# Two query tiles computed with the keys, the values a third tile later, and the conv taps' diagonals written early

## The chip, the cores and the metric

The kernel runs on one core of a Trainium2 chip. The metric is the device time in microseconds of one execution; lower is better. Every matrix product is done in fp32r with operands split in a high and a low part: three matmuls (high by high, high by low, low by high) for each product.

## The reference, cut to what matters

The program is two transformer blocks one after the other, on 256 tokens of width 1024 (the first block also carries 256 context tokens). The first block has two layers: a convolution layer and an attention layer. What the change touches is the attention layer's input side and the convolution's taps:

```
hx = rmsnorm(x, norm_g[i, 0]) * (1.0 + sc_x) + sh_x
hc = rmsnorm(ctx, norm_g[i, 0]) * (1.0 + sc_c) + sh_c
qx = apply_rope(rmsnorm((hx @ wq).reshape(B, S, N_HEADS, HEAD_DIM), q_g), cos, sin)
kx = apply_rope(rmsnorm((hx @ wk).reshape(B, S, N_KV_HEADS, HEAD_DIM), k_g), cos, sin)
kc = rmsnorm((hc @ wk).reshape(B, L, N_KV_HEADS, HEAD_DIM), k_g)
vx, vc = hx @ wv, hc @ wv
...
u = lax.conv_general_dilated(u, w_dw[:, None, :], ..., feature_group_count=u.shape[-1]) + b_dw
```

There are 16 query heads (1024 columns, eight tiles of 128) and 4 key and value heads (256 columns each). Keys and values are made from all 512 tokens, queries from the 256 of x alone.

## The kernel before, in words

**Weights.** All weights come as one stream of pieces of 128 by 1024 fp32 (512 KB), in an order written out in `stream_blocks`. SyncE loads them into seven buffers (`raw`). Pieces of ordinary weights are split: ScalarE copies a piece to fp32r (`whi`, `hi_to`, L1240), then VectorE (`lo_to`, L1908) or GpSimd (L2876, in four operations of 256 columns) writes the rest (`wlo`). `on_pool` decides which of the two, by the piece's turn and by the tile it belongs to. There are five buffers of each part, so a piece can be converted only when the piece five turns earlier has been used up by TensorE (`wdone`). A `raw` buffer is free once the low part is written. Pieces of `w_mod` (the modulation, names such as A, T0, T1) are not split; TensorE reads them from `raw` (L591), and a piece gives its buffer back then. `mod("A")` in the stream is 12 such pieces.

**The attention layer's input.** VectorE and ScalarE make the modulated normalised input k by k, for eight slices of the width: VectorE L2084 (scale), ScalarE L1314 (high part `Hh`), VectorE L2094 (low part `Hl`); VectorE also writes the last additions of the residual there (L2072), and GpSimd adds them to X (L2907). TensorE's `lin_first` (L513, L514: the two products with the high part; L519: the product with the low part) takes each k as soon as it is there, for several output tiles at once. In the kernel before it does so for the two key tiles, `("k", 0)` and `("k", 1)`, 512 tokens wide. Then `lin_tok` (L566 to L568) computes the values for four tiles of tokens. Then the keys' mean squares (`head_sums`, L623), then the eight query tiles, 256 tokens wide, one after the other (`q_lin`, L540 to L542), with the keys' reciprocal roots spread over 128 rows (`head_spread`, L858) behind the first of them, and small matmuls for the queries' mean squares (`q_sums`, L877) between the others.

**Leaving PSUM.** ScalarE's `head` copies a tile to SBUF (L1491 for a key, L1493 for a query) and squares it (L1495). VectorE scales the keys (`scaled`, L2319), turns keys and queries (`rope1`: L2324, L2325, L2327, L2329), and writes the low parts (L2359 for K1l, `q_lo` L2341); ScalarE writes the high parts (L1518 for K1h, `q_hi` L1500). GpSimd copies K1h and K1l to the other half of the partitions (L2922), after its last `wlo` of the queries. The softmax's row maxima on VectorE (L2399) stand in its queue behind the low part of query 7. Matrix products use five PSUM banks in turn.

**The convolution.** TensorE applies 30 taps of four of the eight channel tiles by diagonal 32 by 32 matrices (L767). GpSimd writes these (L2900) in four chunks of up to eight taps; there are three buffers, and the fourth chunk waits until TensorE has used the first.

Of the kernel before, what the change touches and what calls it, by code (L numbers as in the profile page):

```python
# [49 lines left out]
def stream_blocks():  # L50
# [201 lines left out]
def build(nc, wstream, vecs_d, const_d, xin, out):  # L252
# [13 lines left out]
    with ctx:  # L266
# [60 lines left out]
        slots.place(-1, "conv", "bank", range(4, 8), [b[:, :] for b in banks[4:8]])  # L327
        slots.place(0, "dg", "dg", range(3), [DG[:, i, :, :, :] for i in range(3)])
        slots.place(0, "rt", "rt", range(2), [rtb[:, i, :] for i in range(2)])
# [97 lines left out]
        def on_pool(s):  # L427
            tag = turn_tag.get(s, "")
            if s in [tile_turn[key] + 5 for key in (("wo2", 0, 7), ("wo2", 1, 7), ("down2", 0, 1, 7))]:
                return True  # L430
            if tag == "wo" and s <= tile_turn["q", 7] + 5:
                return False
            if tag in ("wo", "wo2", "down2"):
                return True
            if tag == "q":
                return s % 3 != 2
            if tag in ("z", "ya", "gate", "mz", "mb"):
                return s % 3 == 0
            if tag == "up2":
                return s % 3 == 2  # L440
            return False
# [30 lines left out]
        def tensor(e):  # L472
# [22 lines left out]

            def lin_first(keys, kt, src, n, high, low, until=None, between=lambda k: None, idle=0):
                got = [bank("pm", ("lin",) + key, *(until(key) if until else [("ev",) + key])) for key in keys]
                warm(got[0], idle)
                for k in range(kt):
                    xh, xl = src(k)  # L500
                    held = []
                    for ti, key in enumerate(keys):
                        p, o, last = block("w")
                        hi, lo = (x[:, turn_of[p] % NPIECE, o:o + 128] for x in (whi, wlo))
                        turn_tag.setdefault(turn_of[p], key[0])
                        for key_ in keys:
                            tile_turn[key_] = turn_of[p]
                        held.append((p, last, hi))
                        dst = got[ti][:, 0:n]
                        w.wait_ge(*on("lo", p))  # L510
                        for point in high(k):
                            w.wait_ge(*on(*point))
                        e.matmul(dst, hi, xh, start=k == 0, stop=False)  # L513
                        e.matmul(dst, lo, xh, start=False, stop=False)  # L514
                    for point in low(k):
                        w.wait_ge(*on(*point))
                    for ti, key in enumerate(keys):
                        p, last, hi = held[ti]
                        i = e.matmul(got[ti][:, 0:n], hi, xl, start=False, stop=k == kt - 1)  # L519
# [32 lines left out]

            def lin_tok(key, kind, n, tiles, src, xon, until):
                got = [bank("pm", ("lin", key, s), *until(s)) for s in range(tiles)]
                for k in range(8):
# [8 lines left out]
                    for s in range(tiles):  # L564
                        xa, xb = xh[:, s * 128:(s + 1) * 128], xl[:, s * 128:(s + 1) * 128]
                        e.matmul(got[s][:, 0:n], xa, hi, start=k == 0, stop=False)  # L566
                        e.matmul(got[s][:, 0:n], xb, hi, start=False, stop=False)
                        i = e.matmul(got[s][:, 0:n], xa, lo, start=False, stop=k == 7)  # L568
                        points = ([("wdone", p)] if last and s == tiles - 1 else []) + ([("lin", key, s)] if k == 7 else [])
                        if points:  # L570
                            i.then_inc(sig("pe_lin", *points), 1)


# [184 lines left out]
            for i_ in range(CONV_PE):  # L758
                c, q = i_ // CHUNK, i_ % CHUNK
                w.wait_ge(*on("dg", c))  # L760
                dg = DG[:, c % 3, :, :, :]
                for ct in range(4):
                    if i_ == 0:
                        w.wait_ge(*on("u", 4 + ct))
                    for r in range(4):
                        rows = slice(32 * r, 32 * r + 32)
                        i = e.matmul(two(got[r][32 * ct:32 * ct + 32, :]), dg[rows, ct, q, :], U[rows, 4 + ct, :, i_:i_ + T],  # L767
                                     start=i_ == 0, stop=False)
# [78 lines left out]

            def head_sums(key, n):
                b = bank("pst", ("stat", key), ("root", key))
                w.wait_ge(*on("sq", key))  # L850
# [14 lines left out]
            q_done = {}  # L865

# [362 lines left out]
        def scalar(e):  # L1229
# [252 lines left out]
            for k in range(8):  # L1482
                modulated("n2", 1, 0, 2, k)


# [15 lines left out]

            hi_to(("k", 0))
            for m in range(2):
                head(("k", m), 512)
            hi_to(("v",), 3)
            for m in range(2):
                root(("k", m), 8, ("wide", ("k", m)))
            for s in range(4):
# [3 lines left out]
            for j in range(8):  # L1512
                hi_to(("q", j))
                head(("q", j), T)
                if j == 2:
                    for m in range(2):
                        w.wait_ge(*on("roped", ("k", m)))
                        e.activation(K1h[:, 2 * m, :], slots.at(("hr", ("k", m))), ACT.Copy).then_inc(sig("act_q", ("k1h", m)), 1)  # L1518
                if j >= 2:
                    q_hi(j - 2)  # L1520
            w.wait_ge(*on("sums", "q"))
# [374 lines left out]
        def vector(e):  # L1896
# [446 lines left out]

            lo_to(("k", 0))
            lo_to(("v",), 3)
            for m in range(2):
                widen(("k", m), 512)
            for j in range(8):
                lo_to(("q", j))
                if j == 0:  # L2350
                    for m in range(2):
                        scaled(("k", m), 512, "attn_k_g")
                elif j == 1:
                    for m in range(2):
                        rope1(("k", m))
                elif j == 2:
                    for m in range(2):
                        w.wait_ge(*on("k1h", m))
                        e.tensor_tensor(K1l[:, 2 * m, :], slots.at(("hr", ("k", m))), f32(K1h[:, 2 * m, :]), ALU.subtract).then_inc(  # L2359
                            sig("dve_q", ("k1l", m)), 1)  # L2360
                if j >= 2:
                    rope1(("q", j - 2))
                if j >= 2:
                    q_lo(j - 2)
            rope1(("q", 6))
            q_lo(6)
# [496 lines left out]
        def gpsimd(e):  # L2863
# [30 lines left out]
            for c, (i0, n) in enumerate(CHUNKS):  # L2894
                for u in slots.take(0, "dg", ("dg", c), ("dgused", c)):
                    w.wait_ge(*u)
                dg = DG[:, c % 3, :, :, :]
                taps = vec("conv_w_dw", i0 * 8, n * 8).rearrange("p (q k) -> p q k", k=8)
# [224 lines left out]
```

## Time and profile before

| | |
|---|---|
| median of 3 runs | 1968.23 us (1968.08 to 1978.76) |
| profiled execution | 1963.36 us |
| its span, first to last instruction | 1961.1 us |
| TensorE busy | 1884.1 us, 96% of the span |
| VectorE, ScalarE, GpSimd busy | 1204.8, 956.5 and 525.0 us |
| mean granted TensorE clock | 0.992 of full speed |
| stage from the first key matmul to the first softmax maximum | 623.13 to 692.03 us |

The span is what the rows of the trace are counted in, from the first instruction; the profiled execution's time is 2.3 us longer than its span. TensorE is the engine of which the others are the servants here: what matters is when it stands, and who was late.

### The profile page before, as it was taken

How to read it: one execution, taken by the hardware profiler on the slowest of the kernel's cores; microseconds unless marked ns; L12 is line 12 of the kernel's file. 1: busy time of each engine (PE TensorE's matmuls, PEld its weight loads, DVE VectorE, ACT ScalarE, POOL GpSimd, SP SyncE). 2: the span in 40 equal slices, each digit the busy share in tenths (PEclk: the TensorE clock that was granted, in tenths of full speed). 3: DMA queues.
4: the chain of work that ended last, by engine and by line, in shares of the span. 5: the costliest groups of instructions: out<-in, count | busy, mean ns of one | idle time of the engine just before them, and what ended most of it. 6: DMA issues, size and time to landing. Idle time of an engine off the chain costs nothing.

```text
span 1961.1 us, 36041 instructions
## 1 busy us (share of the span) xinstructions
PE 1884.1 (96%) x14682; PEld 1666.9 (85%) x14682; DVE 1204.8 (61%) x2444; ACT 956.5 (49%) x1713; POOL 525.0 (27%) x668
## 2 busy tenths in 40 slices
PE   6999999999998989999998999999999899999998
PEld 3866778888885847899987989999999899999997
DVE  4998753233338575655578675685748876567474
ACT  4314532232233476544446564565655556456464
POOL 1110100000001443000011322647373322374736
PEclk9999999999999999999999999999999999999999
DMA  9345442222224255555544344555554544545551
GB/s 351 127 151 182 143 161 97 97 97 97 97 97 161 87 206 196 200 184 183 183 161 173 130 138 160 173 165 177 190 175 151 173 150 130 171 151 178 185 178 63
DMA packets 84547, 307.24 MB, mean 157 GB/s; under 512 B 9376, under 2 KB 10656, under 8 KB 84128
## 3 DMA queue, kind: packets, MB, share of 16 engines
q1 hardware_dynamic: 84384, 304.94, 45.9%
q8 instruction: 117, 1.92, 0.4%
q14 instruction: 46, 0.38, 0.1%
HBM read 303.86 MB, written 1.05 MB: 155 GB/s over the span
## 4 chain that ended last, share of the span: by engine, by line
PE 82%; DVE 9%; ACT 4%; issue 2%; DMA 1%; POOL 1%; SPq 0%; ACTq 0%; DVEq 0%; POOLq 0%
PE pb L540 18%; PE pb L542 17%; PE pb L541 17%; PE pb L513 6%; PE pb L514 6%; PE pb L519 6%; DVE wlo L1908 2%; PE pb L767 2%; DMA raw<-wstream 1%; ACT whi L1240 1%; PE pb L591 1%; POOL wlo L2876 1%; PE pb L927 1%; PE pb L1111 1%; PE pb L1124 1%
## 5 line engine op out<-in xcount | busy, mean ns | idle before, releaser
L540 PE MATMUL pb<-Hh,whi 128*128 128x256 f32 (+1 forms) x2304 | 699.6, 304 | 1.8 <-DVE SM L2501 1.6
L542 PE MATMUL pb<-Hh,wlo 128*128 128x256 f32 (+1 forms) x2304 | 692.5, 301 | 0.0
L541 PE MATMUL pb<-Hl,whi 128*128 128x256 f32 (+1 forms) x2304 | 692.5, 301 | 0.0
L1240 ACT ACTIVATE whi<-raw 128x1024 fp32r<-128x1024 f32 x468 | 489.7, 1054 | 319.4 <-PE pb L542 177.2
L1908 DVE TENSOR_TENSOR wlo<-raw,whi 128x1024 fp32r<-128x1024 f32 x328 | 424.5, 1298 | 346.4 <-ACT whi L1240 345.9
L2876 POOL TENSOR_TENSOR wlo<-raw,whi 128x256 fp32r<-128x256 f32 x560 | 418.1, 780 | 706.2 <-ACT whi L1240 705.3
L540 PEld LDWEIGHTS pb<-Hh,whi 128*128 128x128 f32 x2304 | 440.0, 191 | 23.0 <-DVE SM L2501 2.5
L541 PEld LDWEIGHTS pb<-Hl,whi 128*128 128x128 f32 x2304 | 440.2, 191 | 15.0
L542 PEld LDWEIGHTS pb<-Hh,wlo 128*128 128x128 f32 x2304 | 440.1, 191 | 15.0
L513 PE MATMUL pb<-Hh,whi 128*128 128x256 f32 (+1 forms) x528 | 162.6, 328 | 3.8 <-ACT Hh L1314 3.4
L514 PE MATMUL pb<-Hh,wlo 128*128 128x256 f32 (+1 forms) x528 | 160.0, 323 | 0.0
L2907 POOL TENSOR_TENSOR X<-X,tmpb 128x512 f32<-128x512 f32 x14 | 18.0, 1290 | 473.5 <-DVE tmpb L2072 473.5
L513 PEld LDWEIGHTS pb<-Hh,whi 128*128 128x128 f32 x528 | 103.2, 196 | 18.9 <-issue 8.9
L519 PE MATMUL pb<-Hl,whi 128*128 128x256 f32 (+1 forms) x528 | 106.7, 324 | 4.0 <-DVE Hl L2094 4.0
L514 PEld LDWEIGHTS pb<-Hh,wlo 128*128 128x128 f32 x528 | 103.2, 195 | 6.8
L519 PEld LDWEIGHTS pb<-Hl,whi 128*128 128x128 f32 x528 | 82.3, 194 | 14.1 <-DVE Hl L2094 6.9
L1875 ACT ACTIVATE tmpb<-pb,VEC 128x256 f32<-128x256 f32 x88 | 48.4, 564 | 79.1 <-PE pb L542 73.3
L2153 DVE SCALAR_TENSOR_TENSOR Y<-U,VEC,Y 128x512 f32<-128x512 f32 x120 | 81.8, 758 | 1.8 <-ACT Y L1355 1.8
L2835 DVE SCALAR_TENSOR_TENSOR tmpb<-pb,VEC,tmpb 128x255 f32<-128x255 f32 x88 | 42.3, 481 | 56.6 <-ACT tmpb L1875 55.6
L1450 ACT ACTIVATE tmpb<-pb 128x512 f32<-128x512 f32 (+1 forms) x44 | 21.1, 491 | 110.6 <-PE pb L542 97.3
L591 PE MATMUL pb<-raw,csz 128*32 128x512 f32 x384 | 52.9, 633 | 20.2 <-DMA raw<-wstream 19.6
L2270 DVE TENSOR_TENSOR tmpb<-pb,tmpb 128x512 f32<-128x512 f32 (+1 forms) x44 | 24.1, 557 | 59.8 <-PE pb L542 49.6
(335 smaller groups left out, 2956.5 us busy)
## 6 DMA issues: line engine op xcount, KB each, us to landing
raw<-wstream SPq DMA_DIRECT2D x572, 512.0 KB, 3.6
X<-xin SPq DMA_DIRECT2D x2, 1024.0 KB, 8.3
out<-X SPq DMA_DIRECT2D x8, 128.0 KB, 1.8
CON<-consts SPq DMA_DIRECT2D x1, 926.0 KB, 8.4
VEC<-vecs SPq DMA_DIRECT2D x1, 662.0 KB, 8.8
CON<-consts SPq DMA_DIRECT2D x1, 147.0 KB, 3.9
VEC<-vecs SPq DMA_DIRECT2D x1, 88.0 KB, 2.0
```

The costliest lines, as they stand in the source:

```text
L513: e.matmul(dst, hi, xh, start=k == 0, stop=False)
L514: e.matmul(dst, lo, xh, start=False, stop=False)
L519: i = e.matmul(got[ti][:, 0:n], hi, xl, start=False, stop=k == kt - 1)
L540: e.matmul(dst, hi, xh, start=k == 0, stop=False)
L541: e.matmul(dst, hi, xl, start=False, stop=False)
L542: i = e.matmul(dst, lo, xh, start=False, stop=k == kt - 1)
L591: i = e.matmul(dst[32 * c:32 * c + 32, :], csz[:, 4 * half + c, o:o + 32], raw[:, p % NRAW, (c % 2) * 512:(c % 2 + 1) * 512], start=m == h ...
L1240: e.activation(whi[:, s % NPIECE, :], raw[:, p % NRAW, :], ACT.Copy).then_inc(sig("act_hi", ("hi", p)), 1)
L1875: e.activation(t[:, s * T:(s + 1) * T], slots.at(("lin",) + key)[:, 0:T], ACT.Identity, scale=vec("ffn_conv_w_2", l * 132 + 88 + c), bias= ...
L1908: e.tensor_tensor(wlo[:, i, :], raw[:, p % NRAW, :], f32(whi[:, i, :]), ALU.subtract).then_inc(sig("dve_lo", ("lo", p)), 1)
L2153: e.scalar_tensor_tensor(out=y, in0=u, scalar=wt, in1=y, op0=ALU.mult, op1=ALU.add).then_inc(sig("dve_conv", *points), 1)
L2876: last = e.tensor_tensor(wlo[:, i, c:c + 256], raw[:, p % NRAW, c:c + 256], f32(whi[:, i, c:c + 256]), ALU.subtract)
```

## The change

Three things change.

1. The two first query tiles are computed in `lin_first` together with the keys, k by k; they take part with the first 256 of the 512 columns (`short`). Query tile 2 follows, then the mean squares of the keys, then the values, then query tiles 3 to 7. The keys' roots are spread inside the values' matmuls, behind their second k, instead of behind query 0. The stream's order is changed to match: keys and queries 0 and 1 in four pieces, then the 12 pieces of A, then query 2, the values (two pieces), queries 3 to 7. The queues of ScalarE and VectorE follow: ScalarE converts the pieces of query 2, the values and query 3 between the eight high parts of the input.
2. A third buffer for squares (`hq`), and the piece of query 2 is never GpSimd's.
3. The diagonals have a buffer for all four chunks, so GpSimd writes the fourth behind the third without a wait.

```
-    run([("attn_wk", (0,), m * 128) for m in range(2)], 2)
+    wq = [("attn_wq", (0,), m * 128) for m in range(8)]
+    group([("attn_wk", (0,), m * 128) for m in range(2)] + wq[:2])
+    mod("A")
+    group(wq[2:3])
     cols("attn_wv", (0,), 0, 256, 256)
-    mod("A")
-    run([("attn_wq", (0,), m * 128) for m in range(8)], 1)
+    for t in wq[3:]:
+        group([t])
...
-        U, DG = overlay(("U", [128, 8, 2, 286], F32), ("DG", [128, 3, 4, CHUNK, 32], F32))
+        U, DG = overlay(("U", [128, 8, 2, 286], F32), ("DG", [128, 4, CONV_PE, 32], F32))
...
-        scratch(2, hr=[1, 2, 3, 4, 7, 8], hq=[9, 10], wide=[5, 6])
+        scratch(2, hr=[1, 2, 3, 4, 7, 8], hq=[9, 10, 0], wide=[5, 6])
...
             if tag == "q":
-                return s % 3 != 2
+                return s % 3 != 2 and s != tile_turn["q", 2]
...
             def lin_first(..., short=()):
+                        c = T if key in short else n
-                        e.matmul(dst, hi, xh, start=k == 0, stop=False)
-                        e.matmul(dst, lo, xh, start=False, stop=False)
+                        e.matmul(dst, hi, xh[:, 0:c], start=k == 0, stop=False)
+                        e.matmul(dst, lo, xh[:, 0:c], start=False, stop=False)
...
TensorE:
-            lin_first([("k", m) for m in range(2)], 8, H2, 512, hh("n2"), hx("n2"), idle=4)
-            lin_tok("v", "w", 256, 4, H2, hx("n2"), lambda s: [("vh", s)])
-            for m in range(2):
-                head_sums(("k", m), 512)
-            q_lin(0)
-            for m in range(2):
-                head_spread(("k", m), 512)
-            q_lin(1)
+            early = [("q", 0), ("q", 1)]
+            lin_first([("k", 0), ("k", 1)] + early, 8, H2, 512, hh("n2"), hx("n2"), idle=4, short=early)
+            q_lin(2)
+            head_sums(("k", 0), 512, "pst")
+            head_sums(("k", 1), 512, "pt")
+            lin_tok("v", "w", 256, 4, H2, hx("n2"), lambda s: [("vh", s)], between=key_spreads)
             q_sums(0)
-            for j in range(2, 8):
+            q_sums(1)
+            for j in range(3, 8):
                 q_lin(j)
                 q_sums(j - 1)
...
ScalarE:
             for k in range(8):
                 modulated("n2", 1, 0, 2, k)
+                if k in (1, 4, 6, 7):
+                    hi_to(("k", 0), (1, 4, 6, 7).index(k) + 1)
...
             for m in range(2):
                 head(("k", m), 512)
-            hi_to(("v",), 3)
+            for j in range(2):
+                head(("q", j), T)
             for m in range(2):
                 root(("k", m), 8, ("wide", ("k", m)))
+            head(("q", 2), T)
+            hi_to(("k", 0), 6)
+            (high parts of the keys, then the values out of PSUM)
+            q_hi(0)
+            for j in range(3, 8):
                 hi_to(("q", j))
                 head(("q", j), T)
...
VectorE:
+            lo_to(("k", 0), 3)
             for m in range(2):
                 widen(("k", m), 512)
+            rope1(("q", 0))
+            for m in range(2):
+                scaled(("k", m), 512, "attn_k_g")
+            lo_to(("k", 0), 4)
+            for m in range(2):
+                rope1(("k", m))
+            lo_to(("k", 0), 6)
+            rope1(("q", 1))
+            (low parts of the keys)
+            q_lo(0)
+            for j in range(3, 8):
                 lo_to(("q", j))
+                rope1(("q", j - 1))
+                q_lo(j - 2)
...
GpSimd, for each chunk c of taps:
-                dg = DG[:, c % 3, :, :, :]
+                dg = DG[:, :, i0:i0 + n, :]
```

## Rows read from the trace of the kernel before

**Rows 1.** Busy time by window: us, each engine's busy time, granted clock, DMA share, GB/s.
```profile
623.00:641.00 18.00, 12.89 (x48) 8.38 (x48) 15.70 (x38) 7.40 (x17) 6.48 (x5) 1.00 0.08 29
655.00:686.00 31.00, 29.09 (x242) 28.52 (x241) 24.20 (x53) 14.65 (x33) 17.67 (x20) 1.00 0.27 86
```
**Rows 2.** TensorE's waits from 622 to 692 us: us in total, times, longest.
```profile
PE pb L519 <- DVE Hl L2094: 4.0, 5, 0.8
PE pb L877 <- ACT tmpb L1495: 1.8, 2, 1.3
```
**Rows 3.** TensorE's timeline, the keys: start, us, and in brackets the idle time before.
```profile
628.96 0.73 PE L519 MATMUL pb<-Hl,whi 128*128 128x512 f32 x2 [0.79 <-DVE Hl L2094]
629.53 0.40 PE L513 MATMUL pb<-Hh,whi 128*128 128x512 f32 x1
629.77 0.39 PE L514 MATMUL pb<-Hh,wlo 128*128 128x512 f32 x1
...
631.41 0.73 PE L519 MATMUL pb<-Hl,whi 128*128 128x512 f32 x2 [0.78 <-DVE Hl L2094]
...
639.37 0.61 PE L519 MATMUL pb<-Hl,whi 128*128 128x512 f32 x2
```
**Rows 4.** VectorE's timeline: the last low parts of the input, the first weight piece.
```profile
636.95 0.87 DVE L2094 SCALAR_TENSOR_TENSOR Hl<-tmpb,MOD,Hh 128x256 fp32r<-128x256 f32 x2
638.01 0.88 DVE L2094 SCALAR_TENSOR_TENSOR Hl<-tmpb,MOD,Hh 128x256 fp32r<-128x256 f32 x2 [0.19 <-ACT Hh L1314]
643.84 1.62 DVE L1908 TENSOR_TENSOR wlo<-raw,whi 128x1024 fp32r<-128x1024 f32 x1 [4.95 <-ACT whi L1240]
```
**Rows 5.** TensorE's timeline, values and queries.
```profile
641.20 0.35 PE L566 MATMUL pb<-whi,Hh 128*128 128x256 f32 x1 [1.21 <-ACT tmpb L1495]
...
652.78 0.95 PE L623 MATMUL pb<-CON,tmpb 128*128 128x2 f32 x8
...
655.00 0.36 PE L540 MATMUL pb<-Hh,whi 128*128 128x256 f32 x1
...
657.95 1.95 PE L858 MATMUL pb<-CON,tmpb 128*128 128x128 f32 x16
...
662.60 0.50 PE L877 MATMUL pb<-CON,tmpb 128*128 128x2 f32 x4
662.96 0.36 PE L540 MATMUL pb<-Hh,whi 128*128 128x256 f32 x1
...
685.40 0.61 PE L877 MATMUL pb<-CON,tmpb 128*128 128x2 f32 x4 [0.56 <-ACT tmpb L1495]
```
**Rows 6.** ScalarE's timeline: an input slice, a key's and a query's square, the Exp table.
```profile
630.18 0.91 ACT L1314 ACTIVATE Hh<-tmpb,MOD 128x256 fp32r<-128x256 f32 x2 [1.60 <-DVE tmpb L2084]
...
640.35 0.59 ACT L1495 ACTIVATE tmpb<-pb 128x512 f32<-128x512 f32 x1
...
658.64 0.42 ACT L1495 ACTIVATE tmpb<-pb 128x256 f32<-128x256 f32 x1
...
686.63 1.28 ACT L1250 ACT_TABLE_LOAD   x1
```
**Rows 7.** VectorE's timeline: low parts of queries 5 and 6, the first softmax maximum.
```profile
686.47 0.43 DVE L2341 TENSOR_TENSOR Hl<-tmpb,Hh 128x256 fp32r<-128x256 f32 x1 [0.48 <-ACT Hh L1500]
...
688.84 0.42 DVE L2341 TENSOR_TENSOR Hl<-tmpb,Hh 128x256 fp32r<-128x256 f32 x1 [0.48 <-ACT Hh L1500]
...
692.03 0.68 DVE L2399 TENSOR_REDUCE SM<-pb 128x1 f32<-128x512 f32 x1
```
**Rows 8.** One line's instructions, VectorE's weight pieces: ns min/median/max, first and last start.
```profile
L1908 DVE TENSOR_TENSOR wlo<-raw,whi x328: 1207/1225/7036, 24.3 to 1904.3; 128x1024 fp32r<-128x1024 f32 x164
```
**Rows 9.** The diagonals' use and making (by line, as above); the last key copies (timeline).
```profile
L767 PE MATMUL pb<-U,DG x960: 585/588/614, 123.3 to 166.7; 32*32 32x512 f32 x192
...
L2900 POOL TENSOR_TENSOR DG<-CON,VEC x16: 627/813/5187, 45.0 to 143.1; 128x256 f32<-128x256 f32 x12, 128x192 f32<-128x192 f32 x4
...
673.30 2.44 POOL L2922 CAST K1l<-K1l 64x512 fp32r<-64x512 f32 x2
```

More of the change, by code:

```diff
@@ L327, in build @@
         slots.place(-1, "conv", "bank", range(4, 8), [b[:, :] for b in banks[4:8]])
-        slots.place(0, "dg", "dg", range(3), [DG[:, i, :, :, :] for i in range(3)])
+        slots.place(0, "dg", "dg", range(len(CHUNKS)), [DG[:, :, i0:i0 + n, :] for i0, n in CHUNKS])
         slots.place(0, "rt", "rt", range(2), [rtb[:, i, :] for i in range(2)])
@@ L494, in warm, with lin_first @@
                     e.matmul(dst[:, 0:256], con("ident"), CON[:, coff["ident"]:coff["ident"] + 256], start=True, stop=True)
-            def lin_first(keys, kt, src, n, high, low, until=None, between=lambda k: None, idle=0):
+            def lin_first(keys, kt, src, n, high, low, until=None, between=lambda k: None, idle=0, short=()):
                 got = [bank("pm", ("lin",) + key, *(until(key) if until else [("ev",) + key])) for key in keys]
@@ L507, in lin_first @@
                             tile_turn[key_] = turn_of[p]
-                        held.append((p, last, hi))
-                        dst = got[ti][:, 0:n]
+                        c = T if key in short else n
+                        held.append((p, last, hi, c))
+                        dst = got[ti][:, 0:c]
                         w.wait_ge(*on("lo", p))
@@ L517, in lin_first @@
                     for ti, key in enumerate(keys):
-                        p, last, hi = held[ti]
-                        i = e.matmul(got[ti][:, 0:n], hi, xl, start=False, stop=k == kt - 1)
+                        p, last, hi, c = held[ti]
+                        i = e.matmul(got[ti][:, 0:c], hi, xl[:, 0:c], start=False, stop=k == kt - 1)
                         points = ([("wdone", p)] if last else []) + ([("lin",) + key] if k == kt - 1 else [])
@@ L551, in singles, with lin_tok @@
                     lin([key], kt, src, n, low)
-            def lin_tok(key, kind, n, tiles, src, xon, until):
+            def lin_tok(key, kind, n, tiles, src, xon, until, between=lambda k: None):
                 got = [bank("pm", ("lin", key, s), *until(s)) for s in range(tiles)]
@@ L571, in lin_tok @@
                             i.then_inc(sig("pe_lin", *points), 1)
+                    between(k)
             def mod_half(name, m, half):
@@ L766, in tensor @@
                         rows = slice(32 * r, 32 * r + 32)
-                        i = e.matmul(two(got[r][32 * ct:32 * ct + 32, :]), dg[rows, ct, q, :], U[rows, 4 + ct, :, i_:i_ + T],
+                        i = e.matmul(two(got[r][32 * ct:32 * ct + 32, :]), DG[rows, ct, i_, :], U[rows, 4 + ct, :, i_:i_ + T],
                                      start=i_ == 0, stop=False)
@@ L845, in tensor, with head_sums @@
             widen("r1", 512, ("mt", "n2", 7))
-            def head_sums(key, n):
-                b = bank("pst", ("stat", key), ("root", key))
+            def head_sums(key, n, ring):
+                b = bank(ring, ("stat", key), ("root", key))
                 w.wait_ge(*on("sq", key))
@@ L859, in head_spread, with key_spreads @@
                 i.then_inc(sig("pe_stat", ("spread", key)), 1)
-            lin_first([("k", m) for m in range(2)], 8, H2, 512, hh("n2"), hx("n2"), idle=4)
-            lin_tok("v", "w", 256, 4, H2, hx("n2"), lambda s: [("vh", s)])
-            for m in range(2):
-                head_sums(("k", m), 512)
-            q_done = {}
+            def key_spreads(k):
+                if k == 1:
+                    for m in range(2):
+                        head_spread(("k", m), 512)
             def q_lin(j):
@@ L1511, in scalar @@
                 e.activation(V1[:, s, :, :], b3, ACT.Copy).then_inc(sig("act_v", ("vh", s)), 1)
-            for j in range(8):
+            q_hi(0)
+            for j in range(3, 8):
                 hi_to(("q", j))
                 head(("q", j), T)
[L1515 to L1520, printed above, removed]
+                q_hi(j - 2)
             w.wait_ge(*on("sums", "q"))
```

29 lines of the change are left out of this document (8 added, 21 removed).

## The prediction

> **What bounds the kernel now.** I read the page first (its figures are in the table above). TensorE is busy 96% of the span, and the mean granted clock is 0.992 of full speed, so a gain can come only from places where it stands or is fed too slowly. The windows come next. From 623 to 641 us, where the keys are computed while their input is being made, TensorE is busy 12.89 of 18.00 us while VectorE has 15.70; from 655 to 686 us it is busy 29.09 of 31.00 [rows 1], both at the full clock. The list of waits names the causes: in the keys it waits for VectorE's low parts, later for the squares of the queries [rows 2]; between the two it waits once for the bank of key 0, whose square on ScalarE is late [rows 5].
>
> The keys in detail. Matmuls of 512 columns start 0.235 us apart (629.53 and 629.77) [rows 3]; a k has six, so 1.41 us of work. But the low-part matmuls of two neighbouring k start at 628.96 and 631.41: a step lasts 2.45 us, set by VectorE, and TensorE has 1.04 us to spare in it [rows 3]. The last k starts its low part at 639.37, and VectorE's last low part ends at 638.89 [rows 3, 4].
>
> **Queries 0 and 1 with the keys.** A query tile alone takes 2.95 us (655.00 to 657.95), 24 matmuls of 0.12 us [rows 5]; two take 5.9 us away from later. Per k they add six short matmuls, 0.72 us, to the 1.41: 2.13 us, still under VectorE's 2.45 [rows 3]. So the step stays VectorE's. I laid the eight k out with the low parts' times as they are. The last low parts come faster, at 637.8 and 638.9 [rows 4] (VectorE has finished the residual by then), so there the longer step shows: k 6 ends at 639.1, k 7 at 641.2 instead of 640.0. The queries cost 1.2 us here and save 5.9: **4.7 us**.
>
> ScalarE's four conversions of weight pieces (about 1.05 us each) now stand between the high parts of the input. A high part takes 0.91 us and ScalarE is idle 1.60 us before the next [rows 6], so each fits. They also wait for TensorE: the second needs the first piece used up (after k 1, by my layout at 627.4) and stands at 631.1; the third needs k 3 (632.1) and stands at 635.9; the fourth needs k 5 (637.0) and stands at 638.0. If TensorE were 1 to 4 us later than laid out these waits would hold the next high part; that is the cover. The pieces themselves have landed: the stream has four pieces ahead of A before and after, A's reads are where they were, and the DMA share is 0.08 in this window because all seven buffers are full [rows 1]. SyncE's queue so moves the same number of pieces past the same points. On GpSimd the additions to X stay first.
>
> **Query 2 and the keys' sums ahead of the values.** The values need the banks of keys 0, 1 and queries 0, 1. Before, TensorE stood 1.21 us for key 0's [rows 5]. Now ScalarE has four `head`s to do, from 640.9. A key's square takes 0.59 us and a query's 0.42 [rows 6], the copy ahead of each about as long, with some overlap: 1.0 us a key, 0.75 a query, until 644.4 or so. The square of query 1 takes key 0's buffer (the ring has three), so it also waits for the sums of key 0, behind query 2 on TensorE. TensorE meanwhile does query 2 (641.2 to 644.15) and two sums (about 0.85 us each without their wait: 652.78 to 655.00 is 2.22 us with one wait of 0.4 in it [rows 5]), until 645.85; query 1's bank is free at about the same time. The stall of **1.2 us** goes, and the 0.4 to 0.6 between the sums too, since both squares were done long before. The low parts for query 2 and the values are VectorE's from 638.9. A piece beside GpSimd's took 1.62 us [rows 4], against a median of 1.225 [rows 8]: 640.5, 642.1, 643.7, each before its use at 641.2, 645.85 and 652.
>
> **The values and the key norm.** Values run 11.6 us (641.20 to 652.78), the two spreads 1.7 us (657.95 to 662.60, less a query's 2.95) [rows 5]: unchanged work, 645.85 to 659.1. The spreads need the roots at 648.7; VectorE has them at 646.9.
>
> **Queries 3 to 7.** Two sums of 0.36 (662.60 to 662.96 [rows 5]) and five times 2.95+0.36 lead to 676.3, then the last sum, whose wait of 0.56 stays [rows 5]: TensorE is through at 677.4 instead of 685.9, so **8.5 us** earlier. By parts: 4.7 (keys), 1.2 and about 0.6 (banks, sums), and about 2.0 of the stalls between queries (1.8 us of waits for squares in all, of which 0.56 stays [rows 2, 5], and slower feeding around them). These came from ScalarE standing at a query's high part for VectorE's rope; in the new order three of eight ropes are done or under way when query 3 starts.
>
> **Who starts the softmax.** Its first maximum stands behind query 7's low part on VectorE, at 692.03, and VectorE is a query every 2.37 us with 0.48 us of waiting for ScalarE in each [rows 7]. In the new order the low part is one query further behind the rope, so that wait falls out and a query costs 1.9 us, less than TensorE's 3.3: the end is set by query 7 leaving TensorE at 675.95. From there: square, sums, root (677.8), Exp table (1.28 us [rows 6], 679.3), high and low part of query 6 (680.2), reciprocal, rope, high and low part of query 7: 683.0, **9.0 us** earlier. The scores can start at 679.9, so VectorE sets the end, as before. From the softmax on nothing is changed in order, and all that follows is chained to it: I take the shift as rigid. GpSimd's key copies (they ended at 675.74 [rows 9]) would end at about 672.5, since the piece of query 6 ahead of them is converted at 661.8; the first scores leave them 7.4 us.
>
> **The diagonals.** TensorE goes through 30 taps from 123.3 to 166.7 us, 1.45 us each, so it uses chunk 3 (taps 24 to 29) from 158 us; the chunk's last operation began at 143.1 [rows 9], so nothing is gained. The four operations (0.63 us each undisturbed [rows 9]) move to 54.5, beside VectorE's four pieces from 54.66. The dearest likely case is 0.4 us for a piece [rows 4, 8]; the first of them is ready 1.2 us before use. Zero, at most 1 us lost; a gain is excluded while TensorE stands nowhere for it.
>
> The sum is 9.0 us at VectorE's gate and 8.5 at TensorE's. I take 8.8: span 1961.1 to 1952.3, profiled execution 1963.36 to 1954.6. The median of the runs shown lies 4.9 above the profiled execution; taking the same off it gives 1959.4.
>
> A rule that speaks against this: row first. One VectorE weight piece took 7.04 us against a median of 1.225 [rows 8], and one of the diagonals 5.19 against 0.63 [rows 9]. The Trainium skill, "SBUF — State Buffer", section "SBUF: two separate sides", says that a VectorE operation with two inputs in SBUF and a GpSimd operation share one port pair as an exclusive lock: who starts first keeps it, the other blocks. By that rule which of the two is held depends on who starts first, and only this stage changes that order, since all later engines shift together. By the medians the sum is 9.0; by the rule, with GpSimd first, it is that of rival (a).
>
> **Rivals.**
> (a) *VectorE's pieces are starved.* GpSimd converts query 3 from 639, four operations in a row, just when VectorE writes query 2's and the values' pieces. The price is up to 5.8 us for one piece (7.04 less 1.225 [rows 8]). Query 2's piece has 0.7 us of slack, the values' 3.7: 2 to 5 us of the gain go, and the time is 1961.5 to 1964.5. For it: the longest piece. Against it: the piece that lay beside GpSimd's in this stage took 1.62 [rows 4], and the median is at the undisturbed 1.225, so long ones are rare.
> (b) *The gain doesn't carry through.* If the early softmax is held by TensorE's other inputs (its bites of T0 and T1 are DMA's), or the keys' longer step breaks the pipeline of ScalarE's conversions, 0 to 4 us remain: 1964.5 to 1968.
> (c) *GpSimd becomes the gate, slower than before.* VectorE's ropes now stand closer together, and GpSimd's eight key copies lie beside them. If a copy is held as the diagonal was, it costs 4.6 us (5.19 less 0.63 [rows 9]). Slack is 7.4 us (scores at 679.9) and the gain 9, so the copies must end after 688.9 for a loss: four held ones do that (672.5+18.4 = 690.9). All eight held end at 709.3, 20 us behind that point: 1988. Against it: the copies lay beside ropes before too, and the last two together took 2.44 [rows 9].
>
> **How the numbers follow.** Forecast, 6 to 11 us gained (1957.2 to 1962.2): 0.72. (a): 0.10. (b): 0.11. (c): 0.02. More than 11, if stalls of the softmax's start vanish too: 0.05. A measurement of this kernel can't tell less than about 1%, 20 us, from no change, so nearly all of this is "same": 0.96; faster 0.02; slower 0.02. The range takes in the forecast, (a), part of (b), and on the low side the 4.9 us by which an execution may lie under the median: 1954.5 to 1965.5.
>
> **What would show it.** Right: L519's starts still 2.45 us apart but with L513, L514 and L519 of 256 columns between; the last at about 641; no wait before L566 over 0.3; L623 before it; the first L2399 at 683. Wrong: steps over 2.5 us; ScalarE's L1240 waiting for TensorE with an L1314 behind it; a piece L1908 over 2 us before 645; L907 waiting for GpSimd; or a first maximum at 683 and an end that has moved by less.

## The result

| | before | after |
|---|---|---|
| median of eight executions each, us | 1976.75 (1967.24 to 1984.77) | 1959.24 (1953.45 to 1966.24) |
| ratio, 95% interval | | 0.9945 [0.9918, 0.9972] |
| profiled execution / its span, us | 1963.36 / 1961.1 | 1961.51 / 1959.1 |
| mean granted clock, share of full | 0.992 | 0.988 |
| first key matmul to first softmax maximum, us | 68.90 | 60.11 |
| first softmax maximum to the end of the span, us | 1269.1 | 1275.4 |

The ratio is 10.9 us of 1976.75; the forecast 8.8 (0.9955) lies in its interval. The two medians lie 17.5 us apart, and the two profiled executions 1.85. The stage that the change touches is 8.8 us shorter, as forecast. In the later sets three executions, of 3065.54, 3550.99 and 6426.34 us where no other lasted over 1988, are left out of every ratio, median and count. The rest of this section reads that stage; the other sections settle why three measures of one gain differ so much.

Busy time by window of the kernel after (columns as in [rows 1]): the keys; the queries.

```profile
623.00:641.00 18.00, 17.10 (x92) 14.32 (x93) 17.81 (x41) 10.57 (x20) 7.97 (x6) 1.00 0.06 25
655.00:680.00 25.00, 24.07 (x205) 23.06 (x208) 18.00 (x40) 11.13 (x25) 9.51 (x12) 1.00 0.24 86
```

In the keys TensorE rose from 12.89 of 18.00 us [rows 1] to 17.10, and VectorE from 15.70 to 17.81: both are full now. TensorE's waits in the stage, as [rows 2] of before, from 622 to 684 us:

```profile
PE pb L517 <- ACT Hh L1320: 0.9, 1, 0.9
PE pb L880 <- ACT tmpb L1503: 0.6, 1, 0.6
```

The 4.0 us for VectorE's low parts [rows 2] are gone, and of the 1.8 us for squares the last 0.6 stays. Its timeline (L517, L518, L523 are the keys' three matmuls, L544 to L546 a query's, L570 the values' first, L628 the sums, L862 the spreads, L880 the later sums, L913 the scores):

```profile
629.47 0.98 PE L523 MATMUL pb<-Hl,whi 128*128 128x512 f32 x4
631.92 0.97 PE L523 MATMUL pb<-Hl,whi 128*128 128x512 f32 x4
...
641.11 0.86 PE L523 MATMUL pb<-Hl,whi 128*128 128x512 f32 x4
641.81 0.28 PE L544 MATMUL pb<-Hh,whi 128*128 128x256 f32 x1
...
644.68 1.84 PE L628 MATMUL pb<-CON,tmpb 128*128 128x2 f32 x16
646.38 0.36 PE L570 MATMUL pb<-whi,Hh 128*128 128x256 f32 x1
...
649.33 1.95 PE L862 MATMUL pb<-CON,tmpb 128*128 128x128 f32 x16
...
677.77 0.61 PE L880 MATMUL pb<-CON,tmpb 128*128 128x2 f32 x4 [0.56 <-ACT tmpb L1503]
680.61 0.50 PE L913 MATMUL pb<-K1h,Hh 64*128 64x512 f32 x2
```

The step is still 2.45 us (629.47 to 631.92), with four low-part matmuls in it in place of two [rows 3]. No bracket stands at the values (646.38), where before had 1.21 [rows 5]. ScalarE, the conversions among the input slices and the last square:

```profile
631.50 1.04 ACT L1246 ACTIVATE whi<-raw 128x1024 fp32r<-128x1024 f32 x1
...
636.34 1.04 ACT L1246 ACTIVATE whi<-raw 128x1024 fp32r<-128x1024 f32 x1
637.58 0.91 ACT L1320 ACTIVATE Hh<-tmpb,MOD 128x256 fp32r<-128x256 f32 x2 [0.20 <-DVE tmpb L2093]
...
645.66 0.38 ACT L1503 ACTIVATE tmpb<-pb 128x256 f32<-128x256 f32 x1 [1.00 <-PE pb L628]
```

The conversions fit between the slices and waited for no weight buffer. The square at 645.66 waited 1.00 us until the sums of key 0 gave its buffer back, and held nobody. VectorE (L1917 are the weight pieces, L2350 the queries' low parts):

```profile
639.33 4.58 DVE L1917 TENSOR_TENSOR wlo<-raw,whi 128x1024 fp32r<-128x1024 f32 x3
...
678.06 0.42 DVE L2350 TENSOR_TENSOR Hl<-tmpb,Hh 128x256 fp32r<-128x256 f32 x1 [1.41 <-ACT Hh L1508]
...
680.55 0.42 DVE L2350 TENSOR_TENSOR Hl<-tmpb,Hh 128x256 fp32r<-128x256 f32 x1 [2.08 <-ACT Hh L1508]
...
683.75 0.68 DVE L2406 TENSOR_REDUCE SM<-pb 128x1 f32<-128x512 f32 x1
```

VectorE now stands 1.41 and 2.08 us ahead of the low parts of queries 5 and 6, where it had 0.48 [rows 7]: its own cycle no longer sets the end, only the last query does. GpSimd, the diagonals, its weight pieces and the last key copies:

```profile
44.34 15.48 POOL L2907 TENSOR_TENSOR DG<-CON,VEC 128x256 f32<-128x256 f32 x16 [42.79 <-DMA VEC<-vecs]
...
639.53 5.66 POOL L2883 TENSOR_TENSOR wlo<-raw,whi 128x256 fp32r<-128x256 f32 x4 [3.44 <-ACT whi L1246]
649.44 2.79 POOL L2883 TENSOR_TENSOR wlo<-raw,whi 128x256 fp32r<-128x256 f32 x4 [4.25 <-ACT whi L1246]
...
670.22 1.44 POOL L2929 CAST K1l<-K1l 64x512 fp32r<-64x512 f32 x2
```

The copies end at 671.66, 8.9 us before the first scores (680.61).

What came after the maxima is the other half of the result. Windows from the first maximum to the end of the span, and its first 138 us, of before:

```profile
692.00:1961.10 1269.10, 1225.84 (x10354) 1161.13 (x10346) 812.41 (x1827) 713.37 (x1340) 464.29 (x603) 0.99 0.50 166
692.00:830.00 138.00, 126.27 (x1049) 98.96 (x1042) 84.31 (x204) 91.42 (x182) 41.21 (x32) 0.98 0.57 202
```

and of after:

```profile
683.70:821.70 138.00, 126.49 (x1035) 98.06 (x1035) 83.23 (x203) 90.45 (x181) 41.23 (x32) 0.96 0.56 200
683.70:1959.10 1275.40, 1232.52 (x10354) 1166.58 (x10353) 815.02 (x1827) 713.63 (x1340) 463.08 (x603) 0.98 0.49 165
```

The same 10354 matmuls are busy 6.7 us longer (1232.52 less 1225.84) under a lower granted clock, and the stretch is 6.3 us longer. TensorE's idle time in it is the same, 43.3 and 42.9 us, so no wait explains the difference. Over the whole span a mean clock of 0.992 means about 31 us at 1.2 GHz in place of 2.4 (0.008 of 1961, twice), and 0.988 about 47; 16 us more at half speed are up to 8 us of work not done. That takes back 6.3 of the 8.8 us in this pair.

### The profile page after: what moved, and what is told of

Same layout as the page of the kernel before. It is cut to its first block, busy times and chain, and to the rows that moved or that the text cites. A ratio compares the mean times of both kernels' runs of the same rounds, so it can differ in the third digit from the quotient of the medians.

```text
span 1959.1 us, 36039 instructions
## 1 busy us (share of the span) xinstructions
PE 1889.7 (96%) x14682; PEld 1672.9 (85%) x14682; DVE 1208.8 (62%) x2446; ACT 957.0 (49%) x1713; POOL 515.5 (26%) x660
## 4 chain that ended last, share of the span: by engine, by line
PE 83%; DVE 8%; ACT 4%; issue 2%; DMA 1%; POOL 1%; SPq 0%; DVEq 0%; ACTq 0%; POOLq 0%
PE pb L544 18%; PE pb L546 18%; PE pb L545 18%; PE pb L517 6%; PE pb L523 6%; PE pb L518 6%; DVE wlo L1917 2%; PE pb L771 2%; DMA raw<-wstream 1%; PE pb L596 1%; ACT whi L1246 1%; PE pb L933 1%; POOL wlo L2883 1%; PE pb L1117 1%; PE pb L691 1%
## 5 line engine op out<-in xcount | busy, mean ns | idle before, releaser
L544 PE MATMUL pb<-Hh,whi 128*128 128x256 f32 (+1 forms) x2288 | 697.4, 305 | 1.8 <-DVE SM L2508 1.6
L546 PE MATMUL pb<-Hh,wlo 128*128 128x256 f32 (+1 forms) x2288 | 690.4, 302 | 0.0
L1917 DVE TENSOR_TENSOR wlo<-raw,whi 128x1024 fp32r<-128x1024 f32 x330 | 431.1, 1311 | 337.1 <-ACT whi L1246 336.7
L2883 POOL TENSOR_TENSOR wlo<-raw,whi 128x256 fp32r<-128x256 f32 x552 | 412.0, 782 | 712.2 <-ACT whi L1246 711.2
L544 PEld LDWEIGHTS pb<-Hh,whi 128*128 128x128 f32 x2288 | 439.4, 192 | 23.0 <-DVE SM L2508 2.5
L546 PEld LDWEIGHTS pb<-Hh,wlo 128*128 128x128 f32 x2288 | 439.5, 192 | 15.1
L517 PE MATMUL pb<-Hh,whi 128*128 128x256 f32 (+1 forms) x544 | 165.4, 325 | 5.1 <-ACT Hh L1320 3.6
L518 PE MATMUL pb<-Hh,wlo 128*128 128x256 f32 (+1 forms) x544 | 162.4, 320 | 0.0
L517 PEld LDWEIGHTS pb<-Hh,whi 128*128 128x128 f32 x544 | 105.3, 194 | 20.7 <-issue 9.9
L518 PEld LDWEIGHTS pb<-Hh,wlo 128*128 128x128 f32 x544 | 105.2, 193 | 6.8
L523 PE MATMUL pb<-Hl,whi 128*128 128x256 f32 (+1 forms) x544 | 107.9, 321 | 0.3
L523 PEld LDWEIGHTS pb<-Hl,whi 128*128 128x128 f32 x544 | 84.5, 192 | 8.9 <-DVE Hl L2103 1.3
```

The costliest lines, as they stand in the source:

```text
L517: e.matmul(dst, hi, xh[:, 0:c], start=k == 0, stop=False)
L518: e.matmul(dst, lo, xh[:, 0:c], start=False, stop=False)
L523: i = e.matmul(got[ti][:, 0:c], hi, xl[:, 0:c], start=False, stop=k == kt - 1)
L546: i = e.matmul(dst, lo, xh, start=False, stop=k == kt - 1)
L1917: e.tensor_tensor(wlo[:, i, :], raw[:, p % NRAW, :], f32(whi[:, i, :]), ALU.subtract).then_inc(sig("dve_lo", ("lo", p)), 1)
L2883: last = e.tensor_tensor(wlo[:, i, c:c + 256], raw[:, p % NRAW, c:c + 256], f32(whi[:, i, c:c + 256]), ALU.subtract)
```

## The experiments

All are full kernels with nothing left out. The ratio is to before on the same chip. "Stage" is first key matmul to first maximum, read from one profile.

| run | ratio [95%] | median, us | stage, us |
|---|---|---|---|
| before again (e1) | 0.9992 [0.9966, 1.0019] | 1966.16 | 70.0 |
| attention only (e2) | 0.9938 [0.9918, 0.9958] | 1956.38 | 60.1 |
| diagonals only (e3) | 0.9974 [0.9951, 0.9996] | 1964.51 | 68.8 |
| after again (e4) | 0.9940 [0.9921, 0.9959] | 1956.99 | 60.1 |
| keys' holes filled (e5) | 1.0002 [0.9993, 1.0011] | 1967.74 | 70.0 |
| query 2 behind the values (e6) | 0.9968 [0.9956, 0.9980] | 1960.99 | 62.8 |
| tail reordered (e7) | 0.9955 [0.9943, 0.9967] | 1958.48 | 57.9 |
| diagonals again (e8) | 1.0000 [0.9991, 1.0009] | 1967.32 | 70.0 |
| after, third (e9) | 0.9949 [0.9930, 0.9967] | 1955.17 | 60.1 |
| one early query (e10) | 0.9960 [0.9941, 0.9980] | 1958.83 | 62.4 |
| tail again (e11) | 0.9948 [0.9929, 0.9966] | 1956.03 | 58.0 |
| key spreads late (e12) | 0.9956 [0.9939, 0.9974] | 1957.53 | 62.1 |
| before, two looks (e13, e14) | | 1966.99; 1966.21 | 70.0; 68.6 |
| keys' holes filled again (e15) | 1.0000 [0.9985, 1.0016] | 1968.70 | 70.3 |
| diagonals, third (e16) | 0.9994 [0.9975, 1.0012] | 1966.58 | 68.7 |
| one more idle matmul (e17) | 1.0000 [0.9987, 1.0014] | 1966.13 | 68.9 |
| before, third (e18) | 0.9995 [0.9972, 1.0018] | 1967.35 | 70.0 |

**Which half of the change gains?** e2 is the kernel after with the edits to DG undone, e3 the kernel before with only those; e1 and e4 repeat the two kernels:

```
-  U, DG = overlay(..., ("DG", [128, 3, 4, CHUNK, 32], F32))
+  U, DG = overlay(..., ("DG", [128, 4, CONV_PE, 32], F32))
-  slots.place(0, "dg", "dg", range(3), ...)
+  slots.place(0, "dg", "dg", range(len(CHUNKS)), ...)
```

> The kernel before against itself: how much two sets of runs of the same program differ, and what clock each execution has. Theory A (the change is worth the 8.8 us of its stage, and all else is scatter of the granted clock): ratio 1.000 within about 0.003, clocks between 0.986 and 0.992 as in the runs of the changed kernel. Theory B (the order of before loses clock in its keys, so the change also gains there): mean clocks below those of the changed kernel, and in some traces a stretch at the lower level between 623 and 641 us.

> The change without its diagonals (three buffers, the fourth chunk waits again). Theory A: the first softmax maximum comes 60.1 us after the first key matmul, as in the whole change and against 68.9 before; time ratio about 0.9955. If the diagonals are worth something (Theory C): stage the same, but the first tap matmul to the first key matmul longer than in the whole change by 1 us or more, and a ratio nearer to 1.

> The diagonals' four buffers alone, attention as before. Theory A: stage 68.9 us as before, time the same within 1 us, ratio 1.000 within the interval; GpSimd's fourth chunk at about 54.5 us. Theory C: faster by 1 us or more.

> The whole change again, on the chip on which its parts are timed. Theory A: 8.8 us less than before, ratio 0.9955, equal to the attention part alone within 1 us. Theory B: 12 us or more less, ratio 0.994 or lower, with mean clocks above those of the kernel before.

The attention part alone gives all of the gain: 0.9938 beside 0.9940 for the whole. The diagonals came out at 0.9974, an interval just free of 1, which no step of the prediction has. So they were run twice more:

> The diagonals alone, a second set of runs. Theory D (the fourth chunk, written beside VectorE's taps, makes the slow group): again no execution over a span of 1970 us in 12, ratio 0.997. Theory B (the keys make it): about three of 12 are, and the first set's none was luck; ratio 1.000.

> The diagonals alone, a third set, for the same question. Theory D (the fourth chunk beside the taps makes the slow group): none over 1970 us though before has some. Theories B and E: as many as in before.

1.0000 and 0.9994, both with 1 inside: in these two sets the diagonals are worth nothing that can be measured, as forecast.

**Does it gain because TensorE has no holes in the keys?** Rival: the holes of 0.8 us a step [rows 3] cost clock later on, so filling them with work that nobody uses gains too.

```
-  lin_first([("k", m) ...], ..., idle=4)
+  lin_first([("k", m) ...], ..., idle=4, between=lambda k: warm(banks[7], 2) if k < 6 else None)
```

> The kernel before, with two extra matmuls of the identity behind each of the first six k of the keys (about 0.87 us of the 1.04 us that TensorE has to spare there; their result goes to a PSUM bank that nobody reads). Theory A (the gain is the 8.8 us of work moved under VectorE's steps): stage 68.9 us as before, times as before, ratio 1.000; filling the holes with nothing useful gives nothing. Theory B (the holes cost clock: before has executions 10 us slower than the rest, 13 of 53 so far over a span of 1970 us, and the changed kernel none): the slow group vanishes, mean span down by about 3 to 4 us, ratio about 0.998.

> The kernel before with the holes in the keys filled, again, wanted on a chip on which before has its slow group. Theory B (the holes cost clock): no execution over a span of 1970 us though before has some beside it. Theory E: some here too, as many as in before.

The idle matmuls took their places: the 18 us from the first key matmul of e5 (626.56) are

```profile
626.56:644.56 18.00, 17.43 (x72) 12.96 (x72) 15.47 (x38) 6.82 (x16) 6.39 (x5) 1.00 0.00 1
```

that is 17.43 busy us where the same 18 us of before (623.13 to 641.13) have 12.89, and the time stayed: 1.0002 and 1.0000. What gains is work moved into the holes, not that they are filled.

**What is each move worth?** e6 is the attention part with query 2 streamed and computed behind the values; e10 keeps only query 0 with the keys; e12 does the keys' spreads behind the values.

```
 e6   group([("attn_wk", ...)] + wq[:2]); mod("A")
      cols("attn_wv", (0,), 0, 256, 256)
      group(wq[2:3])
 e10 -group([("attn_wk", ...)] + wq[:2])
     +group([("attn_wk", ...)] + wq[:1]); group(wq[1:2])
     -early = [("q", 0), ("q", 1)]
     +early = [("q", 0)]   # q_lin(1) ahead of q_lin(2)
 e12 -lin_tok("v", "w", 256, 4, H2, ..., between=key_spreads)
     +lin_tok("v", "w", 256, 4, H2, ...); key_spreads(1)
```

> The attention part of the change (three buffers of diagonals), with query 2 behind the values in stream and queues, so that nothing lies between the keys' last matmul and the values but the keys' sums. By the prediction's steps the values' first matmul then waits for ScalarE's four copies and squares, some 1.5 us that query 2 covered: stage 61.5 us instead of 60.1. Rival: the stall before the values was only the keys' square, and with the sums moved it is gone anyway: stage 60.1 us. Theory D (the fourth chunk's wait makes the slow group): this kernel has it too, about one execution in four over the rest by 10 us. Theory B: no slow group, since the holes in the keys are filled.

> The whole change with query 0 alone computed with the keys; query 1 follows as a tile of its own. By the prediction's steps a k is then 1.77 us of TensorE's work under VectorE's 2.45, the last k ends 0.6 us later than the keys alone would instead of 1.2, and 2.95 us of query 1 come behind: stage 60.1 + 2.95 - 0.6 = 62.4 us, time 2.3 us above the whole change. Rival (a gain in the keys that is mostly one of clock or of the first query): stage and time within 0.7 us of the whole change.

> The whole change with the keys' roots spread behind the values instead of inside them. VectorE's scaling, roping and low parts of the keys (some 8 us of work) then start at about 660.5 instead of 650.4 and stand ahead of query 4's weight piece, which TensorE wants at 663. If VectorE's queue has as little room there as the prediction laid out (1.3 + 1.8 + 1.5 us idle up to 662), the stage grows by 3 to 7 us, to 63 to 67 us. Rival: VectorE has room until the end, and the place of the spreads is worth under 1 us.

In e6 the sums, now straight behind the keys, wait for a square, and the values start behind them:

```profile
644.01 1.94 PE L628 MATMUL pb<-CON,tmpb 128*128 128x2 f32 x16 [0.86 <-ACT tmpb L1504]
645.81 0.36 PE L570 MATMUL pb<-whi,Hh 128*128 128x256 f32 x1
```

The stage is 2.7 us longer. By an estimate some 1.7 of it is clock, in the first of the values just behind these sums:

```profile
645.00:647.00 2.00, 2.00 (x17) 2.00 (x17) 0.64 (x4) 2.00 (x7) 1.34 (x2) 0.88 0.73 244
647.00:650.00 3.00, 3.00 (x16) 3.00 (x16) 2.02 (x8) 0.39 (x1) 0.00 (x0) 0.51 0.82 291
```

(0.12 of 2 us and 0.49 of 3), and 1.0 is left for the edit (0.86 is this wait). The ratios say the same with less certainty: 0.9968 against 0.9940 to 0.9955. Removing that stall is worth about 1 us by this estimate, near the 1.2 predicted; how much of the slower clock reaches the end of the stage was not measured apart.

In e10 the stage is 62.4 us, 2.3 more than after, as expected from the half of the 4.7 us that the keys give; in time it is 0.9960 against e9's 0.9949 on the same chip, 2.2 us by the ratios and 3.7 by the medians, with intervals that overlap: the time agrees with the stage but would not show it alone. The first key matmul and the maxima (ns min/median/max, first and last start) from which the stage is read:

```profile
624.23 0.47 PE L518 MATMUL pb<-Hh,whi 128*128 128x512 f32 x1 [0.34 <-ACT Hh L1322]
```

```profile
L2408 DVE TENSOR_REDUCE SM<-pb x32: 678/683/692, 686.6 to 740.4; 128x1 f32<-128x512 f32 x32
```

In e12 the stage is 2.0 us longer, less than the 3 to 7 expected. VectorE had nothing to do meanwhile and took the keys as soon as they were spread:

```profile
659.47 1.64 DVE L2329 SCALAR_TENSOR_TENSOR tmpb<-tmpb,VEC,pb 128x512 f32<-128x512 f32 x2 [9.98 <-PE pb L862]
```

It stood 9.98 us and then had the same work to do with less room; much of that idle time was room it did not need.

**Can the new end be shortened?** VectorE's last chain hangs on query 6's high part, which ScalarE does behind the root and its table load. e7 and e11:

```
 ACT +q_hi(6)
      w.wait_ge(*on("sums", "q"))
     ...
     -q_hi(6)
 DVE +rope1(("q", 7))
      q_lo(6)
     ...
     -rope1(("q", 7))
```

> The whole change, and behind it query 6's high part ahead of the root and the Exp table on ScalarE, query 7's rope ahead of query 6's low part on VectorE. The profile of the changed kernel has VectorE idle for 2.08 us before query 6's low part, and the first softmax maximum behind it. If the maxima are still gated by VectorE, the stage falls from 60.1 to about 57.8 us, and the time by as much (2 us, ratio to before 0.993). Rival: the scores or the Exp table gate then, and less than 1 us comes.

> The reordered tail again, now beside the whole change on one chip. In the first set its stage was 57.9 us and its softmax 0.5 us longer. Theory: 1.7 us less than the whole change (ratio to before 0.9946). Rival, by the first set's times (ratio 0.9955): the softmax or what follows takes all of it back, 0 us.

The first maximum is 2.2 us earlier, and now waits for the scores instead:

```profile
681.29 0.69 DVE L2406 TENSOR_REDUCE SM<-pb 128x1 f32<-128x512 f32 x1 [0.59 <-PE pb L913]
```

But first to last maximum is 54.4 and 54.9 us, where after has 53.9 and 54.3, and the time doesn't tell it from after: 0.9948 beside 0.9949 on one chip. A gain of under 2 us was seen in the stage and not in the time; I don't claim it.

**Why were the first medians so far apart?** Before has executions that last 10 us and more above its others. Beside each group of variants a set of before was run, five sets in all. Counting as long those over 12 us above the fastest of their set, these held 18 of 131 (8 of 34, 0 of 23, 3 of 23, 1 of 22 and 6 of 29); all kernels with the attention part, 1 of 83. The last runs ask whether that belongs to the order of work or to chance, and try to catch one in a profile:

> One more profiled execution of the kernel before, to catch one of its slow group (span over 1970 us; on two of the three chips so far about one in four, on the third none of 34). Theory E: such an execution has VectorE held behind GpSimd in the queries (656 to 670 us, where GpSimd converts three pieces in a row beside the ropes), so the stage from the first key to the first softmax maximum lasts some 78 instead of 69 us. Rival: the stage lasts 69 to 71 and the 10 us lie elsewhere, then by the stretches: start to first tap, to first key, softmax, rest.

> As the look before it: a second chance to have an execution of the slow group in a profile.

> The kernel before with four instead of three idle matmuls ahead of the first convolution product, at about 28 us, and nothing else. Stage 69 to 70 us, ratio 1.000. For the slow group: if it belongs to an order of work (keys, queries, diagonals), this kernel has it as before does, about one execution in five over a span of 1970 us. If it belongs to the exact program of before (where its code or its waits happen to fall), none of 12 here though before has some.

> The kernel before as its own control in the same session: ratio 1.000, and about one execution in five over 1970 us, as in its reference runs. A profile of one of them would show in which stretch the 10 us lie.

e17 adds one matmul that nobody uses ahead of the first block's first product (`idle=3` to `idle=4`): nothing in its time, and none of 12 executions long. But before itself, run as a variant, had none in 12 in e18 and 2 in 23 counting e1's, the diagonals none in 36, the filled keys none in 23. So all kernels with before's order had 2 in 94 as variants and 18 in 131 in the sets beside them: the order alone does not make them as often as the first medians suggested. The record shows one thing of them: 12 of the 18 had a mean granted clock of 0.988 or less, against 13 of the 113 others. A slower clock is in part what they are. It is not all, since at 0.989 the spans of these sets run from 1963.2 to 1977.3 us. No profile caught one, so the rest stays open.

## Why the prediction was wrong in its last step, and right in the stage

**Keys.** Forecast: step 2.45, last k 1.2 us later. Measured: 2.45, and from the first key matmul to the end of the last low part 18.33 us (623.64 to 641.97) against 16.85 (623.13 to 639.98): 1.5 later, for 5.9 saved, so 4.4 us in place of 4.7. Right in the main; e10's stage confirms the price of one query. What bounded the step, VectorE, had room for none of this, and it did not need any: the added work is TensorE's and ScalarE's.

**Query 2 and sums ahead of the values.** Forecast: the stall of 1.21 goes. It went, and e6 brings 0.86 of it back. The pieces took 4.58 us for three, forecast 4.8.

**Queries and end.** Forecast: TensorE through 8.5 us earlier. From the first key matmul its last sums start at 54.13 us, before at 62.27: 8.1. The first maximum was forecast 9.0 us earlier; it comes 8.3 earlier by the clock of the trace (692.03 to 683.75) and 8.8 when each is counted from its own first key matmul, which lay 0.5 later. VectorE sets the end, through query 6's and 7's last parts, as laid out: e7, which shortens just that chain, moves the maximum.

**Diagonals.** Zero forecast; 0.9974, 1.0000 and 0.9994 measured, so nothing beyond the noise in two sets after a first that suggested 0.3%. VectorE's four pieces beside them took 6.04 us (starting at 53.40) where [rows 4] and [rows 8] led me to allow 0.4 a piece over 4.9; no wait of TensorE answers to it.

**The rivals.** (a) no piece in the stage was starved. (b) the gain carried through: in e2, e4 and e9 the time fell by 0.5 to 0.6%. (c) no copy was held; two take 1.44 us.

**What failed** is the step from the stage to the number: "I take the shift as rigid", then "taking the same off it". It has two terms, and both were mis-sized.

- The rest of the span did not shift rigidly. The span was to be 1952.3 and was 1959.1 us, 6.8 more: behind the first maximum the same matmuls ran 6.3 us longer at a lower granted clock, and the first key matmul lay 0.5 later.
- The median was to lie 7.1 us above the span (1959.4 less 1952.3) and lay 0.1 above it (1959.24 less 1959.1). The 4.9 us between a median and its profiled execution leaned on three executions. With eight, before's median stood 13.4 above its profiled execution (1976.75), and after's 2.3 below.

The errors of 6.8 and 7.0 us cancel. That 1959.4 was forecast and 1959.24 measured is luck. The gain was wrong by the same second term: with before's median at 1968.23 a fall by 8.8 us was forecast, and from 1976.75 the median fell by 17.5. A third sentence failed too, that a measurement "can't tell less than about 1%, 20 us, from no change": eight executions of each gave 0.9918 to 0.9972, which leaves out 1, and e4's interval is 0.9921 to 0.9959.

The later, larger sets show what the change is worth. Leaving out the long executions, the mean spans differ by 9.8 us on one chip (1964.6 for 26 of before, 1954.8 for 12 of after) and by 8.6 on another (1962.8 for 23, 1954.2 for 7), around the forecast 8.8. Executions of equal mean clock say so too. At 0.992 the spans average 1962.1 us (18 of before) and 1953.6 (9 of after), at 0.991 1964.4 (42) and 1954.8 (8), at 0.988 1968.8 (13) and 1958.6 (4): 8.5 to 10.2 apart. What the first medians have above that is before's long executions, only in part explained. A small part of the gain is one that the prediction does not have: in five of eleven profiles of before's order the clock fell behind the keys' sums (last section), and there the stage is 9.9 us longer than after's and not 8.8.

## What to carry to other kernels

Where one engine sets the step and another has a hole in every step, work from later that needs the same operands fits in the hole; what it costs is seen at the last steps, where the feeder gets faster, and what it saves is its whole length later. Read such a change between two landmarks of its own stage, since one pair of profiles can differ by as much elsewhere. A single ratio whose interval just misses 1 (0.9974 here) is repeated before it is explained.

## What the runs showed of the hardware

**The granted clock scatters in unchanged work.** The same code after the maxima was granted 0.99 in one execution and 0.98 in another, and the spans of before went from 1961.1 to 1968.4 (e18, mean clock 0.989). The stage has it too. In e1, TensorE's timeline behind the values, and the windows around it:

```profile
655.64 0.95 PE L623 MATMUL pb<-CON,tmpb 128*128 128x2 f32 x8
656.95 1.05 PE L623 MATMUL pb<-CON,tmpb 128*128 128x2 f32 x8 [0.36 <-ACT SM L1261]
657.86 0.36 PE L540 MATMUL pb<-Hh,whi 128*128 128x256 f32 x1
...
659.06 0.41 PE L541 MATMUL pb<-Hl,whi 128*128 128x256 f32 x1
659.28 0.41 PE L542 MATMUL pb<-Hh,wlo 128*128 128x256 f32 x1
```

```profile
657.00:660.00 3.00, 3.00 (x20) 3.00 (x21) 1.19 (x4) 1.96 (x6) 0.00 (x0) 0.73 0.00 0
660.00:664.00 4.00, 4.00 (x30) 4.00 (x30) 2.15 (x2) 2.78 (x5) 3.58 (x4) 0.77 0.00 0
664.00:670.00 6.00, 6.00 (x53) 6.00 (x52) 5.00 (x12) 1.89 (x4) 4.48 (x7) 1.00 0.72 253
```

In the 7 us from 657 TensorE stands nowhere, and is granted 0.73 and 0.77: 0.27 of 3 and 0.23 of 4 us, doubled, are 3.5 us at 1.2 GHz, where matmuls of 256 columns start 0.22 us apart (659.06 to 659.28) and not 0.12. Ahead of it lie only two groups of eight matmuls of 2 columns with a wait of 0.36 us. The kernel before has the same two groups (from 652.78, [rows 5]) and kept its clock [rows 1]. The profiles of before's order divide by this. In the 3 us that begin 34 us behind the first key matmul the granted clock was 0.50 to 0.69 in e1, e8, e13, e15 and e18, whose stages last 70.0 to 70.3 us; it stayed at 1.00 in the profile of before, e3, e14, e16 and e17, with 68.6 to 68.9, and in e5, whose 70.0 us have a slower clock later (0.89 in the 15 us from 673.6). In e6 the clock fell in the same way right behind a group of such sums with 0.86 us of waiting ahead of it. In the eight profiles with the attention part and no wait ahead of these sums (in after at 644.68) it stayed. Since six profiles with the wait kept their clock, the wait does not decide by itself; that its absence protects the clock is possible and not shown, as no run changed it alone. The Trainium skill, "TensorE: Matmul & The Clock Gate", section "What's actually happening", says that the gate goes by how busy the array has been lately, and that the same kernel meets it differently from run to run. The rows of before and e1 agree with the second; for the first they show only that each fall lies behind such sums with a wait.

**VectorE and GpSimd beside each other.** Three VectorE pieces beside GpSimd's four operations took 4.58 us, 1.53 each against a median of 1.226, and GpSimd's four 5.66 against 2.79 for the four at 649.44 with VectorE's pieces out of the way. The Trainium skill, "SBUF — State Buffer", section "SBUF: two separate sides", tells of an exclusive lock by instruction; in these rows both engines are slowed and neither is starved (1.25 times for VectorE, twice for GpSimd). They don't show who held the ports when, so they neither bear out the lock nor speak against it. Beside the 16 diagonals VectorE's four pieces took 6.04 us, and no diagonal more than 1.61, where one had 5.19 before [rows 9]:

```profile
L2907 POOL TENSOR_TENSOR DG<-CON,VEC x16: 628/814/1607, 44.3 to 58.3; 128x256 f32<-128x256 f32 x12, 128x192 f32<-128x192 f32 x4
```
